# Decode keys of a hybrid decoder step: transposed by VectorE in 32x32 blocks and scored in 16 array tiles

## What is computed

```python
kb_past = cache_k[page_table[:, :nb_full * ppb]].reshape(DB, nb_full, MOBA_BLOCK, H, D)
k_mean = jnp.mean(kb_past, axis=2, dtype=jnp.float32)
idx, valid = _moba_select(q, k_mean, nb_full)          # top 3 of s = q . k_mean
s_sel = jnp.einsum('bthd,bhtkld->bhtkl', q, k_sel).astype(jnp.float32) * scale
p = jax.nn.softmax(jnp.concatenate([s_sel, s_own], axis=-1), axis=-1)
out = jnp.einsum('bhtn,bhtnd->bthd', p[..., :K * L], v_sel...)
```

## Time and profile before

| what | value |
|---|---|
| median of three runs | 1180.7 us |
| the profiled execution | 1177.61 us, its span 1175.9 us |
| PE busy | 1077.4 us, 92% of the span |
| DVE, ACT, POOL busy | 569.0, 448.5, 119.2 us |
| PE transposes of keys (L1773) | 512, PE busy 68.5 us |
| copies of turned keys (DVE L1950, ACT L1876) | 64 and 64, busy 44.1 and 38.1 us |

### The profile page before, as it was taken

The page is one execution under the profiler, slowest core; times in us unless marked ns, Lnnn a source line. Parts: engine busy times, 40 slices in busy tenths (PEclk is TensorE's granted clock), DMA queues, the critical chain, the costliest instruction groups (busy, mean ns, idle before and its releaser), DMA issues.

```text
span 1175.9 us, 21203 instructions
## 1 busy us (share of the span) xinstructions
PE 1077.4 (92%) x7577; PEld 921.2 (78%) x7577; DVE 569.0 (48%) x1227; ACT 448.5 (38%) x1002; POOL 119.2 (10%) x225
## 2 busy tenths in 40 slices
PE   2999999998999889999989892899999999999993
PEld 2988876887888667777778782898899899889983
DVE  3253524653665565555646427545344334444435
ACT  5154213332554365555543226233133113313312
POOL 2001210220000122333230000000000000000000
PEclk8899989999999999999999997899999999999997
DMA  4432215324114789999974421222222222222312
GB/s 135 141 104 71 54 37 119 80 63 140 50 47 116 259 272 325 339 313 324 314 209 123 160 81 36 72 81 83 81 72 88 80 80 80 84 79 73 96 54 80
DMA packets 93702, 149.81 MB, mean 127 GB/s; under 512 B 9377, under 2 KB 39590, under 8 KB 93622
## 3 DMA queue, kind: packets, MB, share of 16 engines
q1 hardware_dynamic: 75040, 103.83, 29.0%
q0 software_dynamic: 11968, 39.85, 10.0%
q10 hardware_dynamic: 6614, 5.06, 1.5%
HBM read 141.62 MB, written 7.10 MB: 126 GB/s over the span
## 4 chain that ended last, share of the span: by engine, by line
PE 76%; DVE 9%; issue 5%; ACT 4%; DMA 2%; SPq 1%; POOL 1%; ACTq 1%; POOLq 1%; DVEq 0%
PE ps L398 29%; PE ps L423 18%; PE ps L801 8%; PE ps L406 5%; PE ps L1773 4%; PE ps L1814 2%; DMA kring<-in_cache_k_dram 1%; PE ps L1782 1%; PE ps L817 1%; PE ps L877 1%; PE ps L897 1%; ACT w L322 1%; DVE xn L452 1%; PE ps L1212 1%; PE ps L887 1%
## 5 line engine op out<-in xcount | busy, mean ns | idle before, releaser
L333 DVE TENSOR_TENSOR w<-w,w 128x512 fp32r<-128x512 f32 (+1 forms) x256 | 179.7, 706 | 353.5 <-ACT w L322 352.4
L322 ACT ACTIVATE w<-w 128x512 fp32r<-128x512 f32 (+1 forms) x256 | 156.0, 614 | 403.1 <-PE ps L406 233.2
L423 PE MATMUL ps<-h2T,w 128*128 128x288 f32 x1536 | 209.8, 298 | 4.1 <-DVE h2T L511 1.8
L423 PEld LDWEIGHTS ps<-h2T,w 128*128 128x128 f32 x1536 | 207.1, 189 | 6.9 <-DVE wide L2228 2.4
L398 PE MATMUL ps<-w,hid 128*128 128x512 f32 x768 | 184.7, 390 | 0.0
L398 PEld LDWEIGHTS ps<-w,hid 128*128 128x128 f32 x768 | 144.0, 188 | 29.7
L398 PE MATMUL ps<-w,hT 128*128 128x512 f32 x576 | 148.5, 408 | 1.4 <-ACT ri L722 1.4
L398 PEld LDWEIGHTS ps<-w,hT 128*128 128x128 f32 x576 | 108.2, 194 | 27.0 <-issue 4.6
L801 PE MATMUL ps<-hT,w 128*128 128x288 f32 x768 | 125.3, 308 | 0.0
L801 PEld LDWEIGHTS ps<-hT,w 128*128 128x128 f32 x768 | 105.8, 190 | 11.3 <-issue 10.6
L1773 PEld LDWEIGHTS ps<-ident,kring 128*128 128x128 f32 x512 | 56.5, 140 | 41.3 <-DMA kring<-in_cache_k_dram 19.0
(11 more groups left out here) (317 smaller groups left out, 1243.7 us busy)
## 6 DMA issues: line engine op xcount, KB each, us to landing
kring<-in_cache_k_dram SPq DMA_DIRECT2D x128, 256.0 KB, 4.1
vring<-in_cache_v_dram POOLq DMA_DIRECT2D x128, 256.0 KB, 4.6
w<-in_w_in_dram SPq DMA_DIRECT2D x88, 256.0 KB, 2.9
w<-in_w_up_dram SPq DMA_DIRECT2D x64, 256.0 KB, 2.7
w<-in_w_down_dram SPq DMA_DIRECT2D x64, 256.0 KB, 2.6
w<-in_w_out_dram SPq DMA_DIRECT2D x16, 256.0 KB, 2.6
x<-in_x_prompt_dram SPq DMA_DIRECT2D x4, 512.0 KB, 7.0
out_dram<-sC ACTq DMA_DIRECT2D x1, 2048.0 KB
```

Source lines behind the costliest of these rows:

```text
L322: eng.activation(spread(w_hi, n, j, width), together(w32, n, j, width), ACT.Copy)\
L333: eng.tensor_tensor(spread(w_lo, n, j, width), together(w32, n, j, width), spread(w_hi, n, j, width).bitcast(F32), ALU.subtract).then_inc( ...
L423: mm = eng.matmul(ps[:, b, 0:HALFT], w[a][:, j, i * P:(i + 1) * P], right[c][:, k, h * HALFT:(h + 1) * HALFT], start=(k == 0 and (c, a) == ...
```

## The change

- `keys_turn`, the two ACT copies and the two DVE copies of a group go. DVE turns the group itself, straight from `kring` into `kT`, with one transpose instruction over 128x2048 elements that transposes each 32x32 block within its place. `k_free` is now set by this instruction, which waits for the pages and for the scores of the group before (`kT` has no second buffer).
- Scores are now 64 matmuls of a 32x32 stationary block with 128 columns, in 16 tiles of the array (4 row groups by 4 column groups, 4 accumulating matmuls in each). Row group q takes the tokens 32q to 32q+31 of each page and writes bank 2+q. The queries lie in `qz`, which POOL fills with 16 small copies per sequence: two sequences ahead of decode, the others in POOL's queue ahead of the value pages of a sequence.
- ACT brings the scores to `sS` in two activations per group, which also sum each block into `ssum` by the accumulator; DVE's sum goes, its maximum stays.
- Probabilities are transposed through columns 128 to 255 of banks 2 to 5. `probs_turn(s-6)` therefore waits until the scores of group s-1 have been read out.
- `pieces_in(s)` is 2 in every slot divisible by 4, else 1, and one piece in slots 33 to 38: four pieces move from the finishing slots to slots 0, 8, 16 and 24. The prompt keeps 2 per slot; weight steps are now split in the prompt by the same rule as in decode.
- POOL's loop over sequences is written out, and the load of `g_post_mix` moves behind all scores, because `qz` lies in its buffer.

```diff
-    kT = sb("kT", [P, HP, CH], F32, "R2")
+    kT = sb("kT", [P, 4, HP, 2, 2, 32], F32, "R2")
...
+    def pieces_in(s):
+        if s < ALL_GROUPS:
+            return 2 if s % 4 == 0 else 1
+        return int(ALL_GROUPS < s < ALL_GROUPS + 7)
...
+    def pool_queries(eng, b):
+        if b >= 2:
+            eng.wait_ge(sem("p_S_ps"), GROUPS * (b - 1))
+        for p in range(4):
+            for j in range(2):
+                for f in range(2):
+                    eng.tensor_copy(qz[32 * p:32 * p + 32, b % 2, :, j, f, j * S:(j + 1) * S],
+                                    QTs[64 * j + 32 * f:64 * j + 32 * f + 32, :, b * S:(b + 1) * S])\
+                       .then_inc(sem("p_qz"), 1)
...
-        with eng.Fori(0, B) as b:
+        for b in range(B):
+            if b >= 1 and b + 1 < B:
+                pool_queries(eng, b + 1)
             for g in range(GROUPS):
                 eng.wait_ge(sem("v_free"), b * GROUPS + g + 1)
                 pages(eng, cache_v, vring, "v_in", b, g)
...
         def scores(m):
-            eng.wait_ge(sem("p_kT_act"), 2 * m + 2)
-            eng.wait_ge(sem("p_kT_dve"), 2 * m + 2)
-            eng.wait_ge(sem("p_S"), m)
-            for h in range(HP):
-                mm = eng.matmul(ps[32 * h:32 * h + 32, 4, :], qb[:, (m // GROUPS) % 2, h, :], kT[:, h, :],
-                                start=True, stop=True)
+            eng.wait_ge(sem("k_free"), m + 1)
+            eng.wait_ge(sem("p_S"), 2 * m)
+            eng.wait_ge(sem("p_PT"), max(m + 1 - VALS, 0))
+            if m % GROUPS == 0:
+                eng.wait_ge(sem("p_qz"), 16 * (m // GROUPS) + 16)
+            for u, (j, f) in enumerate(((0, 0), (0, 1), (1, 0), (1, 1))):
+                for q in range(4):
+                    r = slice(32 * q, 32 * q + 32)
+                    for h in range(HP):
+                        mm = eng.matmul(ps[32 * h:32 * h + 32, 2 + q, 0:P],
+                                        qz[r, (m // GROUPS) % 2, h, j, f, :], kT[r, :, h, j, f, :],
+                                        start=(u == 0), stop=(u == 3))
             mm.then_inc(sem("p_S_ps"), 1)
...
         def probs_turn(m):
             eng.wait_ge(sem("p_exp"), 2 * m + 2)
             eng.wait_ge(sem("p_PT"), m)
+            eng.wait_ge(sem("p_S"), 2 * min(m + VALS, ALL_GROUPS))
...
-            eng.activation(sS[:, g * CH:(g + 1) * CH], ps[:, 4, :], ACT.Copy).then_inc(sem("p_S"), 1)
+            for k in range(2):
+                c = slice(g * CH + k * 2 * PAGE, g * CH + (k + 1) * 2 * PAGE)
+                eng.activation(sS[:, c].rearrange("p (j q n) -> p q j n", j=2, n=32),
+                               ps[:, 2:6, 64 * k:64 * (k + 1)].rearrange("p q (j n) -> p q j n", n=32),
+                               ACT.Copy, accum_out=ssum[:, 2 * g + k:2 * g + k + 1]).then_inc(sem("p_S"), 1)
...
+        def keys(m):
+            eng.wait_ge(sem(f"k_in{m % 2}"), 64 * (m // 2) + 64)
             eng.wait_ge(sem("p_S_ps"), m)
-            eng.tensor_copy(kT[:, h, :], ps[:, 3, :]).then_inc(sem("p_kT_dve"), 1)
+            eng.transpose(kT[:, :, :, :, :, :].rearrange("p a h j f n -> p (a h j f n)"),
+                          kring[:, (m % 2) * 4:(m % 2) * 4 + 4, :].rearrange("p a n -> p (a n)"))\
+               .then_inc(sem("k_free"), 1)
```

More of the change, by code:

```diff
@@ L845, in sg_at, with act_gates, dve_branches, sp_step @@
         return sg[:, f * NT + h * HALFT:f * NT + (h + 1) * HALFT]
-    def act_gate(eng, n, u, h):
-        if h == 0:
-            drain(eng, n, 0)
-        else:
-            step_used(eng, UNIT0 + 2 * u + 1)
-        f = (u + KT) % (2 * KT)
-        drained(eng.activation(sg_at(f, h), ps[:, h, 0:HALFT], ACT.Tanh, scale=0.5), n, h)
+    def act_gates(eng, n, g):
+        for p in pieces_of(g):
+            if p < GATE_PIECES and p % 2 == 1:
+                u, h = p // 4, (p % 4) // 2
+                if h == 0:
+                    drain(eng, n, 0)
+                else:
+                    step_used(eng, UNIT0 + 2 * u + 1)
+                drained(eng.activation(sg_at((u + KT) % (2 * KT), h), ps[:, h, 0:HALFT], ACT.Tanh, scale=0.5), n, h)
+            elif p >= GATE_PIECES:
+                skip(n, p % 2, p % 2 == 1)
+    def dve_branches(eng, n, g):
+        for p in pieces_of(g):
+            if p >= GATE_PIECES:
+                branch_out(eng, n, p - GATE_PIECES)
+            elif p % 2 == 1:
+                skip(n, (p % 4) // 2, (p % 4) // 2 == 1)
     def head(h2):
         return slice(h2 * DH, (h2 + 1) * DH)
-    NSLOTS = len(SLOTS)
+    def sp_step(eng, n, r):
+        if r < 4 * KT:
+            f, half = (r // 2 + KT) % (2 * KT), r % 2
+            src = w_in[half * 4 * P:(half + 1) * 4 * P, GA0 + f * P:GA0 + (f + 1) * P]
+        else:
+            f = (r - 4 * KT) % KT
+            src = (w_mlstm_br if r < 5 * KT else w_attn_br)[:, f * P:(f + 1) * P]
+        w_load(eng, n, src.rearrange("(k p) f -> p k f", p=P), 4)
+    def sp_prompt(eng, n):
+        for r in range(AHEAD + 1):
+            sp_step(eng, n, r)
+        for r in range(NSLOT, AHEAD + NSLOT):
+            sp_step(eng, n, r)
+        for g in range(A_SLOTS):
+            if g == 3 * PT:
+                eng.wait_ge(sem("small_in"), 64)
+                eng.wait_ge(sem("a_kT"), HP)
+                eng.wait_ge(sem("a_qT"), HP)
+                eng.wait_ge(sem("kv_out"), 64)
+                pages(eng, cache_k, kring, "k_in", 0, 0)
+                pages(eng, cache_k, kring, "k_in", 0, 1)
+            for r in fetched_in(g):
+                sp_step(eng, n, r)
     def pe_prompt(eng, n, main):
@@ L910, in pe_prompt @@
         turn(0, 1)
-        for s in range(NSLOTS + 1):
-            next(main)
-            next(main)
+        for s in range(A_SLOTS):
+            for _ in range(A_PIECES):
+                next(main)
             if s >= 1:
@@ L957, in act_prompt @@
         eng.wait_ge(sem("m_out"), 48)
-        for s in range(NSLOTS + 1):
+        for s in range(A_SLOTS):
+            act_gates(eng, n, s - 1)
             if s >= 1:
-                act_gate(eng, n, (s - 1) // 2, (s - 1) % 2)
                 turned(s - 1)
@@ L965, in act_prompt @@
                     queries(s // 4 + 1)
+            for _ in steps_in(s):
                 w_high(eng, n)
@@ L1004, in dve_prompt @@
         keys(0)
-        for s in range(NSLOTS + 1):
-            if s >= 1:
-                skip(n, (s - 1) % 2, (s - 1) % 2 == 1)
+        for s in range(A_SLOTS):
+            dve_branches(eng, n, s - 1)
             if s < NSLOTS:
@@ L1833, in pe_decode @@
         for s in range(DSLOTS):
-            for _ in range(2 * pieces_in(s)[0]):
-                next(main)
             if 1 <= s <= ALL_GROUPS:
                 scores(s - 1)
-            if s < ALL_GROUPS:
-                keys_turn(s, 0)
-                keys_turn(s, 1)
+            for _ in range(pieces_in(s)):
+                next(main)
             if VALS <= s < ALL_GROUPS + VALS:
@@ L1868, in act_decode @@
     def act_decode(eng, n):
-        def keys(m, h):
-            if h == 0:
-                eng.wait_ge(sem("p_kT_ps"), 3 * m + 1)
-            else:
-                eng.wait_ge(sem("p_kT_ps"), 3 * m + 3)
-            eng.wait_ge(sem("p_S_ps"), m)
-            eng.activation(kT[:, h, :], ps[:, 2, :], ACT.Copy).then_inc(sem("p_kT_act"), 1)
         def scores(m):
@@ L1927, in act_decode @@
                 out((s - GROUPS - VALS - 1) // GROUPS)
-            if s < ALL_GROUPS:
-                keys(s, 2)
-            for _ in steps_in(s):
+            for _ in steps_in(A_SLOTS + s):
                 w_high(eng, n)
```

139 lines of the change are left out of this document (47 added, 92 removed).

## The result

The changed kernel takes 1218.95 us, median of four runs (1215.1 to 1224.15), against 1181.41 us for the kernel before (four runs on the same chip, 1178.22 to 1183.34): a ratio of 1.032 with an interval of 1.027 to 1.038. It is 37.5 us slower. The prediction, 1167 in a range of 1150 to 1187, was wrong, in sign too.

The account below looks back on a forecast made before the run. In slots 8 to 31 PE and the transfers were both nearly full, so relieving PE would uncover the transfers. Terms -7, -5 and -1.5 sum to -13.5 on the profiled 1177.6, so 1164; with 3.1 for the median 1167, range 1150 to 1187.

Parts of the forecast that it names:

- the price of the scores: PE's 64 score matmuls, 128 records at 9 ns between starts: 1.4 us a group, bounds 1.0 and 4.0.
- the own scores: PE's records of 8 columns in four tiles, 8 per sequence: the source of the 9 ns between starts.
- turning point of 2.6 us: Scores of 2.6 us, 20 ns a record, bring PE's four slots from 23 us to today's 27.9.
- rival 4: PE's queue at the head of every slot: score matmuls bound by issue, about 1217 or 1192 us; chance 0.12.
- something else: Causes outside the named rivals, such as a lower clock in slots 0 to 7; chance 0.06.
- PE's part: Slots 8 to 31: PE needs some 23 us per four slots, 21.5 before waits, 138 us in the stretch.
- The transfers as the wall: Slots 8 to 31: 53.8 MB at 345 GB/s take 156 us; 160 forecast, minus 7.
- rival 2: Slots 8 to 31 gain nothing, engines stay at 0.94 and 320 GB/s: about 1178 us; chance 0.13.
- The 4 us "above the transfers' own time": Slots 8 to 31: an allowance of 4 us over the transfers' 156, where the stretch now has 12.
- DVE and ACT: Slots 8 to 31: turn 2.3 us, DVE about 105 and ACT 77 of 160 us, beside the transfers, costing nothing.
- POOL: Query copies behind value pages make scores wait 2 us six times, 12 in all, inside PE's wait for pages.
- The spread of the pieces: Four pieces leave the finishing slots, 7.4 us of PE: minus 1.5 there; moved pieces cost nothing elsewhere.

Follow-up runs that it names:

- the cut kernel: The kernel before with each score matmul of 512 columns cut into 16 of 32 columns, 128 records a group: 1220.1 us, ratio 1.033.
- half of the scores: The changed kernel with 32 instead of 64 score matmuls per group, one head of each pair left out: 1179.6 us, ratio 1.000.
- The late values: The changed kernel with scores in two bursts of 32 matmuls, a half piece between them, and values a slot later: 1249.1 us, ratio 1.056.
- the filler: The changed kernel with two matmuls that nobody reads at the end of each slot from 6 to 31: 1217.0 us, ratio 1.030.
- the sums alone: The kernel before with block sums by ACT's accumulator in two activations of 256, DVE's sum gone, pieces spread as before: 1183.1 us, ratio 1.001.
- the one at 1175.3: The changed kernel with half of the score matmuls and POOL's copies of queries one group of value pages sooner: 1175.3 us, ratio 0.994.

## Why the prediction was wrong, step by step

**The step that failed: the price of the scores.** The sum took 1.4 us a group from 9 ns a record. Undisturbed it is 1.90 us, (1.90 - 0.27) / 127 = 13 ns from record to record; the 4 ns between starts of different tiles that the prediction also weighed were seen nowhere. The 9 ns of the own scores do hold in four tiles (the cut kernel: 1.30 us for 128), and not quite in sixteen. At 1.90 us PE's pace would still be under the turning point of 2.6 us that rival 4 names. But the bursts last 3.2 us on average, because of stops of 0.4 to 3.4 us between blocks of instructions. Rival 4 gave 1217 for scores of 4.0 us and had the place right (PE's queue at the head of the slots) and by chance the size, with a cause that is not the one found: issue is quick, delivery is late. At the 3.2 us that the bursts did last its own sum gives 1192; the other 27 us are not in that sum, which has no lower clock, no wait for `sg` and no longer finishing slots. The prediction carried a rate read from eight records over to 128 in a row, each with its load of weights, and did not ask where 256 instructions come from. The profile of before had the row: a queue for instructions with 50 packets for 0.82 MB. The change raises PE's instructions in decode from 156 a slot (1873 + 1872 over 24) to 367.

The Trainium skill ("Runtime: NRT & Kernel Launch", section Instruction fetch mechanics) says that instructions are refilled in 16 KiB blocks of 256, and that crossing a boundary is mostly hidden. The blocks agree with the trace; "mostly hidden" holds in the kernel before and for 268 instructions a slot, and not for 367 or 396, where crossings cost 37.3 and 29.7 us.

**The clock.** It had only a part of the 0.06 for "something else". It was low for 58 us of 381 to 635, 53 of them with PE busy, which is up to 27 us of extra time on PE: the second term that the sum lacked. The prediction took 30 us of work from PE in the middle (159.4 less 6 x 21.5), and did not ask whether PE would keep its clock with the gaps. It costs nothing where the transfers are the wall (half of the scores, clock 0.89, time as before), and adds to the stops where PE is late.

**PE's part, about 138 us in the middle.** 129 of them were work (6 x 21.5), the rest waits. The work measured 162.9 us, 34 more. 24 x (1.9 - 1.4) = 12 are the scores; the clock was low for (1 - 0.89) x 2 of 201.6 = 44 us, which is worth up to 22. The forecast of 160 had PE wait for 8 us of these 138 and 22 us for pages. PE was idle for 38.7 us, but for other reasons: 26.4 of stops, 6.4 for `sg`, 4.4 for `qz` and none for pages.

**The transfers as the wall.** Right, and with half of the scores it shows: DMA share 0.95, PE idle a fifth of the stretch. The size was not: 168.4 where 160 was put, 324 GB/s and not 336. The 4 us "above the transfers' own time" were a choice without a row; 12 was what the earlier trace rows had, and it stayed at that. So rival 2 (about 1178) describes what the change would be worth without the cost of its instructions: 1179.6.

**DVE and ACT.** Right in their amounts. The turn is 2311 ns (forecast 2.3), DVE is busy for 107.5 us in the middle (105), ACT for 73.7 (77); both mostly wait for PE. "Cost nothing" was not quite right: the turn stands ahead of DVE's sums for the pieces, and PE waited three times, 6.4 us in all, for `sg`, against once for 0.4 us before. With half of the scores it is 7.5 us, so the stops do not make it. No run has the old order of DVE with nothing else changed.

**POOL.** Right in mechanism: with half of the scores five waits for `qz` of 2.2 us each, against 2 us six times. The copies follow each other every 0.26 us in decode rather than 0.2. That this wait is hidden was nearly right (4.3 of 11.0 us came back when the copies moved). The late values showed how thin the cover is: one slot of delay made of it 39 us.

**The spread of the pieces.** Wrong: -1.5 in the finishing slots and nothing elsewhere were forecast; in the old layout it cost 6.4 us. How much of the 37.5 it makes in the changed kernel was not measured. The finishing slots did not shorten: PE waits there for value pages, whose pace the prediction itself had written down. And the slots that got the pieces were not free.

**What stays open.** How the loss of 37.5 us divides between stops, clock, the waits for `sg` and `qz` and the spread of the pieces is not settled: the filler moved stops and clock at once, and no run leaves the spread out of the changed kernel. The 1179.6 with half of the scores contain the spread too. Why the transfer of a block began anywhere from 0.5 to 5.3 us after PE had entered the block before it isn't known either; the late ones were mostly those behind a stop. And no version that does all of the work beats the kernel before: the sums alone are even with it, and the one at 1175.3 leaves out half of the scores.

## What to carry to other kernels

Count instructions, not only columns: when many small matmuls replace a few large ones, divide PE's matmuls and weight loads by 256 and compare the time per block with what caused no stops and what did (here one block in 6.7 us cost next to nothing, and one in 5, by the pace of the slots before, cost 37 us). Before taking work from an engine that is 95% busy, look at what stands at 94% beside it, since that is what the gain will shrink to, and at the clock, since an engine with gaps may lose it. When an order is rearranged to help one wait, list which waits the moved work had covered, on every queue behind it.

## What was unexpected in the hardware

- PE's instructions arrive in blocks of 16 KB on queue 8. The transfer takes 1.05 us, but two of them never began less than 3.35 us apart in any kernel here, and a stop ends 1.2 to 1.6 us after its block has landed. Taking away nearly half of the page traffic shortens the stops by a third only (37.3 to 25.9 us).
- Sixteen tiles do not start faster than four: undisturbed, 128 records of 32x32 with 128 columns take 1.90 us, 13 ns from record to record, and those of 128x32 with 32 columns in four tiles 1.30 us, 9 ns. The Trainium skill ("TensorE: Matmul & The Clock Gate", Part 1) has a floor of about 25 ns from start to start. No burst here kept to it record by record; if the two records of one float32 matmul are taken as one, the sixteen tiles come to 26 ns and the four to 18.
- Work for PE of 29.4 us that nobody needs left the time unchanged: the clock was low for 25 us instead of 58 of 381 to 635 us, and the stops were shorter by 14.4 us.
